# Two weight units put in the residual tile X, and half of the token copies made by GpSimd

## What is computed

```python
x = x + mixer(rmsnorm(x, norm_mix[i]))
x = x + moe_ffn(rmsnorm(x, norm_ffn[i]), router_w, router_b, w_gate[i], w_up[i], w_down[i])

def moe_ffn(xt, router_w, router_b, w_gate, w_up, w_down):   # 16 experts in 4 groups, 2 experts per token
    scores = sigmoid(xt @ router_w)
    # gates: of the best group the two best experts, normalised
    a = silu(xt @ w_gate[e]) * (xt @ w_up[e]) * gates[e]     # 2048 -> 512
    y = sum_e a @ w_down[e]                                  # 512 -> 2048
```

## Time and profile before

| | |
|---|---|
| median of 3 runs | 1689.19 us (1689.03 to 1690.26) |
| the profiled execution | 1688.99 us, span 1687.3 us |
| granted TensorE clock, mean | 0.999 |
| TensorE matmuls | 1665.3 us busy (99%) |
| VectorE, ScalarE, GpSimd | 748.1 (44%), 485.3 (29%), 54.1 us (3%) |
| loads from HBM | 530.33 MB, mean 316 GB/s |
| expert stages | about 419 to 868 us and 1234 to 1680 us |

### The profile page before, as it was taken

The page is one execution under the profiler, slowest core; times in us unless marked ns, Lnnn a source line. Parts: engine busy times, 40 slices in busy tenths (PEclk is TensorE's granted clock), DMA queues, the critical chain, the costliest instruction groups (busy, mean ns, idle before and its releaser), DMA issues.

```text
span 1687.3 us, 20430 instructions
## 1 busy us (share of the span) xinstructions
PE 1665.3 (99%) x8533; PEld 1057.8 (63%) x8533; DVE 748.1 (44%) x1236; ACT 485.3 (29%) x624; POOL 54.1 (3%) x32
## 2 busy tenths in 40 slices
PE   9999999999999999999999999999999999999997
PEld 8888888887444444444359999988744444444343
DVE  6885477744122222222256777784522222232223
ACT  6444456434000000000054565664330000000000
POOL 3000000100000000000030000020000000000000
PEclk9999999999999999999999999999999999999999
DMA  8755546577899999999994544554799999999997
GB/s 299 256 195 173 195 159 200 172 270 303 360 412 418 428 427 428 427 427 425 421 345 156 152 140 152 202 179 161 294 371 412 416 427 428 428 427 427 427 421 293
DMA packets 114325, 533.80 MB, mean 316 GB/s; under 512 B 12949, under 2 KB 31929, under 8 KB 81209
## 3 DMA queue, kind: packets, MB, share of 16 engines
q1 hardware_dynamic: 113856, 532.32, 80.5%
q10 hardware_dynamic: 344, 0.13, 0.0%
q0 software_dynamic: 32, 0.02, 0.0%
HBM read 530.33 MB, written 2.11 MB: 316 GB/s over the span
## 4 chain that ended last, share of the span: by engine, by line
PE 93%; DMA 4%; DVE 2%; ACT 1%; issue 0%; DVEq 0%; ACTq 0%; SPq 0%
PE PS L736 32%; PE PS L1059 25%; PE PS L1091 12%; PE PS L1021 7%; DMA DOUBLE<-in_moe_w_down 3%; PE PS L847 3%; PE PS L1034 2%; PE PS L1035 1%; PE PS L868 1%; PE PS L853 1%; PE PS L946 1%; PE PS L1200 1%; PE PS L1226 1%; PE PS L1205 1%; ACT AREA L1507 1%
## 5 line engine op out<-in xcount | busy, mean ns | idle before, releaser
L1688 DVE TENSOR_TENSOR LO<-ring,HI 128x2048 fp32r<-128x2048 f32 (+1 forms) x124 | 266.9, 2153 | 167.0 <-ACT HI L1316 166.5
L1059 PE MATMUL PS<-DOUBLE,AREA 128*64 128x512 f32 x1120 | 314.2, 595 | 0.0
L1316 ACT ACTIVATE HI<-ring 128x2048 fp32r<-128x2048 f32 (+1 forms) x124 | 223.6, 1803 | 265.7 <-PE PS L736 239.0
L736 PE MATMUL PS<-HI,XT_BOTH 128*128 128x512 f32 (+1 forms) x1344 | 297.9, 373 | 0.8 <-issue 0.6
L736 PEld LDWEIGHTS PS<-HI,XT_BOTH 128*128 128x128 f32 x1344 | 243.9, 188 | 35.4 <-issue 2.3
L2013 DVE TENSOR_TENSOR X<-PS,X 128x512 f32<-128x512 f32 x128 | 82.1, 684 | 303.4 <-PE PS L1035 303.4
L1059 PE MATMUL PS<-OVD,AREA 128*64 128x512 f32 x448 | 200.1, 595 | 0.0
L1059 PEld LDWEIGHTS PS<-DOUBLE,AREA 128*64 128x64 f32 x1120 | 95.6, 137 | 147.8 <-issue 147.3
L1091 PE MATMUL PS<-DOUBLE,AREA 128*64 128x512 f32 x672 | 171.0, 596 | 6.4 <-DMA DOUBLE<-in_moe_w_down 4.9
L736 PE MATMUL PS<-LO,XT_BOTH 128*128 128x512 f32 (+1 forms) x672 | 152.5, 368 | 0.0
L2022 DVE TENSOR_TENSOR AREA<-PS,VFF 128x512 f32<-128x512 f32 x64 | 44.2, 691 | 205.9 <-PE PS L1021 205.9
(11 more groups left out here) (294 smaller groups left out, 1732.9 us busy)
## 6 DMA issues: line engine op xcount, KB each, us to landing
DOUBLE<-in_moe_w_gate SPq DMA_DIRECT2D x30, 2048.0 KB, 18.7
ring<-in_a_w_in SPq DMA_DIRECT2D x48, 1024.0 KB, 5.2
DOUBLE<-in_moe_w_up SPq DMA_DIRECT2D x22, 2048.0 KB, 18.2
DOUBLE<-in_moe_w_down SPq DMA_DIRECT2D x22, 2048.0 KB, 19.6
DOUBLE<-in_moe_w_down SPq DMA_DIRECT2D x40, 1024.0 KB, 9.9
OVD<-in_moe_w_down SPq DMA_DIRECT2D x12, 2048.0 KB, 19.1
ring<-in_b_w_in SPq DMA_DIRECT2D x32, 768.0 KB, 4.4
DOUBLE<-in_moe_w_up SPq DMA_DIRECT2D x20, 1024.0 KB, 9.4
```

The lines of the kernel that those rows point to most:

```text
L736: mm = pe.matmul(PS[:, banks[t], 0:n], lhs(k0 + kk, t)[part], weights[:, kk, 0:n], start=first and kk == 0 and p == 0, stop=last and kk == ...
L1059: last = pe.matmul(PS[64 * e:64 * e + 64, up, :], m_["XG"][:, c, 64 * e:64 * e + 64], slot(units[e])[:, kk, :], start=(c == 0), stop=(c == ...
L1316: act.activation(HI[s % 2][:, :, 0:n], ring[PLACE[u]][:, :, 0:n], ACT.Copy).then_inc(sem("hi_ready"), 1)
L1688: tt(LO[PLACE[u]][:, :, 0:n], ring[PLACE[u]][:, :, 0:n], HI[s % 2][:, :, 0:n], ALU.subtract)\
```

## The change

- **A place in X.** `ONCE` becomes 4: units 20 and 21 are loaded into X, as one double of 2 MB, once all copies from X to XN are made. X is not read again before pair 1, where `first_block` writes each of its eight blocks anew from XN, times the root SSQ[:, 4:6], plus the scattered result. `before_in_slot` shifts with it: unit k follows k-22, then k-20 for 38 and 39, and k-18 from 40 on.
- **The copies.** ScalarE makes four of the eight copies (the first 1024 columns), GpSimd the other four by `tensor_scalar` (`xn_rest`), after it has waited for `logits` and `ffn_norm`.
- **Scatters** go to banks 2, 3 and 4, 5 in turn, and two of them stand together after the first step of each half instead of one after each of steps 1, 3, 5 and 7. The last pair waits for all adds before its transposes.
- **The opening of pair 6** (its first 8 matmuls) moves in front of the end of the branch, and carries the counts that stood behind a drain.
- `keep_on` reads constants instead of X.

```diff
-ONCE = 2
+ONCE = 4
...
-    return k - EARLY if k < 2 * WIDE else k - WIDE
+    return k - EARLY if k < EARLY + WIDE - 2 else k - EARLY + 2 if k < EARLY + WIDE else k - WIDE
...
-        return k if k < WIDE - ONCE else k + ONCE if k < WIDE else (k - ONCE) % WIDE
+        return k if k < WIDE - 2 else k + 2 if k < WIDE else k - 2 if k < WIDE + 2 else k if k < EARLY else (k - ONCE) % WIDE
...
+SCATTER_BANKS = (2, 4, 2, 4)
...
+        x_at = top[0]
+        DOUBLE[WIDE + 2] = at(f"DOUBLE{WIDE + 2}", x_at, [P, 2, UNIT_K, UNIT_C])
...
-                u = base + EARLY - ONCE
+                u = base + WIDE
-                src = list(expert_sources(*gate_rows(layer), down_rows(layer), 0))[(EARLY - ONCE) // 2]
+                src = list(expert_sources(*gate_rows(layer), down_rows(layer), 0))[WIDE // 2]
...
                 else:
                     early_half(13)
                     early_half(15)
+                sp.wait_ge(sem("xn_ffn"), 4 * layer + 4)
+                sp.wait_ge(sem("xn_rest"), 4 * layer + 4)
+                early(WIDE + 2)
                 all_of = [src for i in range(PAIRS) for src in expert_sources(wg, wu, wd, i)]
...
             sp.wait_ge(sem("stored"), 16 * 5)
 
 
+        def rows_of_eight(t, g):
+
+            q, k = g // 2, UNIT_K * (g % 2)
+            return (XN[:, t, UNIT_C * g:UNIT_C * (g + 1)].rearrange("p (k j) -> p k j", k=UNIT_K),
+                    X[:, t, :].rearrange("p (q j k) -> p q k j", q=2, k=2 * UNIT_K)[:, q, k:k + UNIT_K, :])
+
         @block.gpsimd
         def _(pool):
...
                         pool.tensor_tensor(XTL[:, 4 * g:4 * g + 4, :], b_["OT"][:, 4 * g:4 * g + 4, :],
                                            XTH[:, 4 * g:4 * g + 4, :], ALU.subtract).then_inc(sem("ot_ready"), 1)
 
+                pool.wait_ge(sem("logits"), l + 1)
+                pool.wait_ge(sem("ffn_norm"), 2 * l + 1)
+                for g in range(2, 4):
+                    for t in range(NT):
+                        to, of = rows_of_eight(t, g)
+                        pool.tensor_scalar(to, of, SSQ[:, 6 + t:7 + t], None, ALU.mult).then_inc(sem("xn_rest"), 1)
                 pool.wait_ge(sem("routed"), l + 1)
                 flag = pool.value_load(FLAG[0:1, l:l + 1], min_val=0, max_val=1)
...
-                    pe.matmul(PS[:, bank, 0:n], ONES, X[:, 0, 0:n], start=True, stop=True)
+                    pe.matmul(PS[:, bank, 0:n], ONES, CON[:, 0:n], start=True, stop=True)
...
-                            pe.wait_ge(sem("xn_ffn"), 8 * l + NT * (g + 1))
+                            pe.wait_ge(sem("xn_ffn" if g < 2 else "xn_rest"), 4 * l + NT * (g % 2 + 1))
...
 
                     pe.wait_ge(sem(m + "y_low"), 4 * j + d + 1)
                     for t in range(NT):
-                        bank = FINAL_BANKS[d] + t if final else 2 + t
+                        bank = FINAL_BANKS[d] + t if final else SCATTER_BANKS[d] + t
                         if d > 1 and final:
                             pe.wait_ge(sem("x_final"), 8 * l + 2 * d + t - 3)
-                        elif d > 0 and not final:
-                            pe.wait_ge(sem(m + "x_added"), 8 * (j - l) + 2 * d + t - 1)
+                        elif d > 1 and not final:
+                            pe.wait_ge(sem(m + "x_added"), 8 * (j - l) + 2 * d + t - 3)
                         pe.matmul(PS[:, bank, :], SCT[:, t * P:(t + 1) * P], YH[:, d, :], start=True, stop=False)
                         pe.matmul(PS[:, bank, :], SCT[:, t * P:(t + 1) * P], YL[:, d, :], start=False, stop=True)\
                             .then_inc(sem(m + "scattered"), 1)
 
-                def pair(m, j, g, following, arrived, slot, consumed, whole, prev, first=False):
+                def opening(m, g, arrived, slot, consumed, left_out=()):
+
+                    pe.wait_ge(sem(m + "xg_ready"), 4 * g + 4)
+                    arrived(0)
+                    arrived(2)
+                    for c in range(UNIT_K):
+                        for e in range(2):
+                            last = pe.matmul(PS[64 * e:64 * e + 64, 0, :], m_["XG"][:, c, 64 * e:64 * e + 64],
+                                             slot(2 * e)[:, c, :], start=(c == 0), stop=False)
+                            if c == UNIT_K - 1:
+                                last.then_inc(consumed, 1)
+                            else:
+                                for name, total in left_out[2 * c + e:2 * c + e + 1]:
+                                    last.then_inc(sem(m + name), total)
+
+                def pair(m, j, g, following, arrived, slot, consumed, whole, prev, first=False, opened=False):
 
 
                     def finished(mm, n):
                         mm.then_inc(consumed, 1)
 
-                    if not first:
+                    if not first and not opened:
...
                                 if first and up == 0:
                                     pe.wait_ge(sem(m + "xg_ready"), 4 * g + 2 * q + k + 1)
                                 units = [8 * q + 4 * up + 2 * e + k for e in range(2)]
-                                for n in units:
+                                here = not (opened and q == up == k == 0)
+                                for n in units if here else ():
                                     arrived(n)
-                                for kk in range(UNIT_K):
+                                for kk in range(UNIT_K if here else 0):
                                     c = 8 * q + UNIT_K * k + kk
                                     for e in range(2):
                                         last = pe.matmul(PS[64 * e:64 * e + 64, up, :], m_["XG"][:, c, 64 * e:64 * e + 64],
                                                          slot(units[e])[:, kk, :], start=(c == 0), stop=(c == DC - 1))
                                         if kk == UNIT_K - 1:
                                             finished(last, units[e])
-                                if k == 0 and prev and (following or 2 * q + up < 3):
-                                    scatter(m, j - 1, 2 * q + up)
+                                if k == 0 and up == 0 and prev:
+                                    scatter(m, j - 1, 2 * q)
+                                    if following or q == 0:
+                                        scatter(m, j - 1, 2 * q + 1)
                     if following:
                         if prev:
                             pe.wait_ge(sem(m + "x_added"), 8 * (j - l))
                         gather(m, following, (0, 1))
                     elif prev:
                         scatter(m, j - 1, 3)
+                    if prev and not following:
+                        pe.wait_ge(sem(m + "x_added"), 8 * (j - l))
                     pe.wait_ge(sem(m + "a_ready"), 2 * j + 2)
                     for c in range(FC):
...
                                                                   16 * (PAIR_UNITS // 4) * k + 16 * (order(n) // 4 + 1)),
                                  lambda n: OV[order(n) % 4], sem(f"over_free_{l}"), False, False)
                     gather(m, gather_turn(l, MIDDLE))
+                    u0 = base + PAIR_UNITS * MIDDLE
+                    opening(m, gather_turn(l, MIDDLE), lambda n: unit_arrived(pe, u0 + n), lambda n: in_double(u0 + n), used)
 
...
                         home = nc.cur_bb
                         pe.br_cmp(flag, 0, on_true=f"pe_over_{l}", on_false=f"pe_plain_{l}", comp_op="IS_GT")
                         nc.switch_bb(f"pe_plain_{l}", parent=home)
-                        pe.drain()
-                        for name, total in OVER_PE:
-                            pe.sem_inc(sem(m + name), total)
+                        opening(m, gather_turn(l, i), arrived, lambda n: in_double(u0 + n), used, OVER_PE)
                         pe.br(f"pe_joined_{l}")
                         nc.switch_bb(f"pe_joined_{l}", parent=home)
                     if i == MIDDLE - 1:
...
@@ -1139,7 +1177,7 @@
                     last_one = i == PAIRS - 1
                     ahead = 0 if last_one else LAYER_GATHERS * l + i + 1 if i < MIDDLE else gather_turn(l, i + 1)
                     pair(m, pair_turn(l, i), gather_turn(l, i), ahead, arrived, lambda n: in_double(u0 + n), used, True,
-                         i > 0, i == 0)
+                         i > 0, i == 0, i == MIDDLE)
 
                 for d in range(1, 4):
...
@@ -1493,12 +1531,10 @@
                 for t in range(NT):
                     act.activation(m_["SC"][:, t, :], PS[:, 7, N_EXP * t:N_EXP * (t + 1)], ACT.Sigmoid, scale=SSQ[:, 6 + t:7 + t])\
                         .then_inc(sem("scores"), 1)
-                for g in range(4):
-                    q, k = g // 2, UNIT_K * (g % 2)
+                for g in range(2):
                     for t in range(NT):
-                        act.activation(XN[:, t, UNIT_C * g:UNIT_C * (g + 1)].rearrange("p (k j) -> p k j", k=UNIT_K),
```

(31 more changed lines are left out.)

## The result

The changed kernel takes **1698.07 us** (median of 11 executions, 1694.19 to 1702.44) where the kernel before, timed beside it, takes 1689.61 (11 executions). The ratio is 1.0053, with a 95% interval of 1.0045 to 1.0061: some 9 us slower. 1694.7 was predicted. The profiled execution has a span of 1696.7 us at a mean granted clock of 0.995 (before 1687.3 and 0.999).

The account below looks back on a forecast made before the run. Expert stages were taken as bound by TensorE and the load queue, the end of pair 1 fixing each stage's end. 3.6 + 3.3 - 0.7 - 0.7 = +5.5 us on a 1689.19 us median gave 1694.7 us, range 1687 to 1701.

Parts of the forecast that it names:

- The kernel's bound and the sign: Expert stages: TensorE and load queue both bind, end of pair 1 fixes the stage's end; slower overall, chance 0.62.
- The port wait, +3.6 and +3.3: Routing, layers 0 and 1: GpSimd's copies hold VectorE's chain through shared ports, delaying the mask by these us.
- the prediction's own rule: Routing: VectorE's first, second, third and fifth chain operations each end with one GpSimd copy, taken as 1.27 us.
- the 0.4 us a layer: Routing: GpSimd's next copies also wait for VectorE operations that slipped in; half of up to 0.8 us, each layer.
- The likeliest case: Routing: VectorE held at the ports while TensorE's clock stays up; 1692.5 to 1697.5 us, chance 0.38.
- rival 1: Before the mask: TensorE's idle time also lowers its clock, in one layer or both; 1697 to 1703 us, chance 0.25.
- the sum of +5.5: Whole kernel, us: 3.6 + 3.3 for the routing less 0.7 per layer for merged scatters, giving 1694.7.
- The scatters, -0.7 per layer: Expert pairs: merging scatters saves 0.7 us a pair, counted only in pair 1, so once per layer.
- that dry moment: End of pair 1, about 534: the load queue runs empty (319 GB/s; 295 in layer 1), then never pauses.
- The place in X, 0: Load queue: units 20 and 21 loaded early save nothing, since units 62 and 63 still await pair 1's end.
- Rival 3: Load queue: the two early units stay in hand, last landing 4.9 us earlier per layer; about 1686 or 1680, chance 0.15.
- Covered costs: ScalarE's halved copies, the load into X, reordered first adds and the last pair's wait for adds: each taken as 0.

Follow-up runs that it names:

- e2: Kernel before with only GpSimd's four copies added; place in X, scatters and opening as before: 1699.74 us, ratio 1.0062.
- e5: Changed kernel, with GpSimd's four copies waiting until the routing is done: 1689.35 us, ratio 1.0002.
- e6: Changed kernel with three more 512-column filler matmuls on TensorE before the mask: 1694.58 us, ratio 1.0036.
- e11: Changed kernel with GpSimd's four copies reading neighbouring columns instead of steps of eight (output not the reference's): 1693.07 us in a single execution.
- e4: Kernel before with only the merged scatters and the moved opening of pair 6: 1689.26 us, ratio 1.0001.
- e7: Kernel before with double loads from unit 80 on instead of unit 56, single loads until then: 1688.94 us, ratio 1.0003.
- e3: Kernel before with only the place in X added; copies on ScalarE, scatters as before: 1691.27 us, ratio 1.0013.
- e12: Kernel before with the place in X, all copies on ScalarE, and double loads only from unit 80 on: 1687.79 us, ratio 0.9987.
- e1: Changed kernel with all eight copies back on ScalarE; place in X and merged scatters kept: 1689.14 us, ratio 0.9997.
- e8: Kernel before with merged scatters, the moved opening of pair 6, and double loads only from unit 80 on: 1689.04 us, ratio 1.0001.
- e9: Changed kernel with all copies on ScalarE and double loads only from unit 80 on: 1686.67 us, ratio 0.9988.

## Why the prediction was right, and where it was off

**The kernel's bound and the sign.** Right. A delay before pair 0 is passed on whole (e2), and from some 127 us after the logits the queue never pauses (426 to 428 GB/s in both kernels). Slower was forecast, by the port wait of the routing; e5 shows that the copies cost only beside the routing, and the timelines show VectorE held there. (That it is a port they wait for is the Trainium skill's account; the traces show only who is held and how long.)

**The port wait, +3.6 and +3.3.** Measured +3.27 and +2.98 at the gather, and 6.1 us by e6's ratio against 6.9. The size came out nearly right although the copy was taken for 1.27 us and took 2.05, and that is in part luck. By the prediction's own rule, each held operation ends with its copy, four copies of 2.05 us would give 414.1 + 8.2 - 415.96 = 6.3 us. Two errors cancelled: the copy was longer, and it held VectorE only for its first 1.23 us. My picture was off in more ways. The chain operations held are the first, the fifth and two later ones (L2005, L2013), since the second to fourth run behind the held part of the first copy; so one hold lies behind the mask, which is only 2.31 and 2.03 us late. Reading two tensors in SBUF is not the condition: L2005 reads one, and was held for 0.90 us. And the 0.4 us a layer for GpSimd waiting in its turn was not there: its four copies take 8.18 us beside the chain and 8.20 behind it (e5). In the Trainium skill (SBUF — State Buffer, "SBUF: two separate sides") one engine has the ports for its whole instruction while the other is blocked. The earlier trace rows agree with that; the copies don't: VectorE was shut out for 1.23 of 2.05 us, and for 0.73 of 1.55 in e11. The 1.24 us that the prediction worked out as an estimate from the Trainium skill's GPSIMD Engine Reference ("Performance pitfalls for Q7 kernels") is near the held part and not near the whole copy.

**The clock: the step that failed.** The likeliest case kept the clock, because the stretches before and after are full. It fell, in both layers, at 2.58 and 2.56 us of waiting, the value from which rival 1 was said to decide, and cost 2.23 and 0.72 us (e6). As a boundary that value doesn't hold (it stayed after 2.84 us in e11, and fell after 2.08 in the changed kernel), so that it fell in both layers was not certain. So rival 1 (0.25) is what happened, at 1697 to 1703 with 1698.07 measured, and the likeliest case's own range (to 1697.5) ends just below. The prediction even priced the idle time at 3.9 us, well beyond its own 2.6, which should have given rival 1 the larger chance. (3.9 was itself too long, since one hold lies behind the mask.) Against the measured +9.0 the sum of +5.5 lacks the clock's 2.95 us, takes off 1.4 us for scatters that the time doesn't show, and has the port wait 0.65 us too high.

**The scatters, -0.7 per layer.** Pairs are 0.75 us shorter as forecast; at the end of layer 0 and 1 e4 has -1.0 and -0.35; in the time nothing is to be seen (e4, 1.0001). The reason given, that the end of pair 1 fixes the end of the stage, is too narrow: in e7 that dry moment is gone and the stage ends as it did.

**The place in X, 0.** It costs about 2 us behind double loads (e3) and pays behind single ones (e12 against e7, 0.9987 against 1.0003). Rival 3 (it pays, 4.9 us a layer) was wrong for this kernel; one constant away the place pays some 2 us in all, a fifth of that.

**Covered costs.** ScalarE's halving was worth nothing; the load into X was hidden; the first adds take 1.11 us against 0.68 and, like the 1.23 us wait for the adds in the last pair, cost nothing that e1 shows. By the runs' parts the sum is 6.1 (e6's ratio) + 2.95 (the clock, by the timelines) + about 0 for place and scatters (e1) = 9.05, and 9.0 was measured.

**Left open.** In layer 1 of the changed kernel the last weights are 5.51 us later, more than the 3.70 by which pair 0 starts later; the queue's tail is longer there. And its executions spread over 8 us, those of before over 4; its two slowest (1702.44 and 1701.30) have a mean granted clock of 0.994 and 0.993, its quickest (1694.19) 0.996, so the time at 1.2 GHz may differ from one to the next, but only one was traced.

## What to carry to other kernels

Before giving work to GpSimd, look at what VectorE does in that moment: beside a chain of short dependent operations each GpSimd copy of the changed kernel held one for 0.3 to 0.95 us, and the same work placed behind the chain cost nothing. Price a delay on TensorE's path together with the clock, as a chance and not as a rule: ahead of the gather it fell to 1.2 GHz after all four gaps of 2.6 us, for 3.4 to 6.8 us, but behind waits for weights of 2.1 to 2.8 us it fell in four cases and stayed in four. Room for more loads in advance paid here only where the loads that followed took single units, and then little.

## What the runs showed of the hardware that I had not expected

- A GpSimd scaled copy of 128x512 float32 took 2.05 us reading in steps of eight elements and 1.55 plain, and held VectorE's operation for its first 1.23 and 0.73 us, the rest of 0.82 us not at all; one that read a single tensor (L2005) was held too.
- The granted clock did not fall during TensorE's wait but some 0.4 us (layer 0) and 0.7 us (layer 1) after it had ended, as worked out from the means of 0.71 in 419 to 420 and 0.81 in 1238 to 1239, and was at 1.2 GHz until about 426.3 and 1242.0, well into the gather.
- It fell after a wait of 2.08 us (773.08) and stayed after one of 2.84 (e11, 1655.87).
- Loads of 1.05 MB moved 424 to 425 GB/s over 60 us (127 to 187 us after the logits in e7, e8, e9, e12) where loads of twice the size moved 425 to 429 in the other runs.
- A VectorE operation on 128x512 that adds PSUM to a scaled SBUF tile read in another order took 1.11 us where the plain add took 0.68.
